# Two distances between the chunks of a matmul operand in SBUF: 2048 and 2080 bytes

## The reference

```python
def ada_in(h, g, m, j):
    xn = rms_norm(h, g)
    return xn * (1.0 + m[:, j, 1][:, None]) + m[:, j, 0][:, None]

def swiglu(x, w_in, w_out):
    a, b = jnp.split(x @ w_in, 2, axis=-1)
    return (jax.nn.silu(a) * b) @ w_out

# second_block, for each of its 2 layers (kind = retention, then neighbourhood attention)
h  = gated_residual(h,  ml, 0, swiglu(ada_in(h,  norm_g[i, 0], ml, 0), ffn_w_in[i, 0], ffn_w_out[i, 0]), 0.5)
hc = gated_residual(hc, mc, 0, swiglu(ada_in(hc, norm_g[i, 0], mc, 0), ffn_w_in[i, 0], ffn_w_out[i, 0]), 0.5)
xl, xc = ada_in(h, norm_g[i, 1], ml, 1), ada_in(hc, norm_g[i, 1], mc, 1)
yl, yc = mixer(xl, xc, ...)          # its input projections are x @ w_in or x @ w_qkv
h  = gated_residual(h, ml, 1, yl, 1.0)
# hc likewise, and a second swiglu, in the last layer for h alone
```

## The kernel before, in words

| | before | remainder by 256 | after | remainder by 256 |
|---|---|---|---|---|
| `xhi`, chunk 0 | 32896 | 128 | 32896 | 128 |
| `xlo`, chunk 0 | 49280 | 128 | 49536 | 128 |
| `raw` and `wlo` | 65664 | 128 | 66176 | 128 |
| `whi` | 82048 | 128 | 82560 | 128 |
| `arena0` (`ghi`, `fhi`, ...) | 129152 | 128 | 130944 | 128 |
| chunk k of `xhi` in block 2 | 32896 + 2048 k | 128 for all k | 32896 + 2080 k | 128 + 32 k, less 256 from k = 4 on |
| chunk k of `xhi` in block 1 | 32896 + 1088 k | 128, 192, 0, 64, 128, ... | same | same |

## Time and profile before

### The profile page before, as it was taken

The page is one execution under the profiler, slowest core; times in us unless marked ns, Lnnn a source line. Parts: engine busy times, 40 slices in busy tenths (PEclk is TensorE's granted clock), DMA queues, the critical chain, the costliest instruction groups (busy, mean ns, idle before and its releaser), DMA issues.

```text
span 3107.7 us, 48774 instructions
## 1 busy us (share of the span) xinstructions
PE 3051.3 (98%) x17714; PEld 2594.2 (83%) x17714; DVE 1880.8 (61%) x3622; ACT 1272.3 (41%) x2142; POOL 204.7 (7%) x350
## 2 busy tenths in 40 slices
PE   9999999999999999999999999999999999999999
PEld 7677899975779998888888888888888888786999
DVE  5555656654567576555676556755557555656554
ACT  4546565343665643222332452322223222336443
POOL 0000000000000010000010000011110111023000
PEclk9999999999999999999999999999999999999999
DMA  5222356622225573444453114445554555462454
GB/s 181 83 76 81 124 174 196 215 95 75 82 89 173 185 238 129 145 148 143 136 190 109 55 62 138 130 150 151 155 161 135 155 158 156 152 178 62 150 182 156
DMA packets 122711, 431.18 MB, mean 139 GB/s; under 512 B 16176, under 2 KB 19504, under 8 KB 122048
## 3 DMA queue, kind: packets, MB, share of 16 engines
q1 hardware_dynamic: 93776, 336.28, 33.0%
q0 software_dynamic: 26880, 86.47, 10.1%
q10 hardware_dynamic: 1904, 6.36, 0.5%
HBM read 427.99 MB, written 8.85 MB: 141 GB/s over the span
## 4 chain that ended last, share of the span: by engine, by line
PE 66%; DVE 1%; ACT 1%; DMA 1%; issue 0%; DVEq 0%; SPq 0%; ACTq 0%
PE ps L429 18%; PE ps L430 18%; PE ps L431 18%; PE ps L510 1%; PE ps L512 1%; PE ps L511 1%; PE ps L922 1%; PE ps L460 1%; PE ps L465 1%; PE ps L461 1%; PE ps L898 1%; PE ps L525 1%; DMA raw<-in_panels 1%; PE ps L981 0%; PE ps L924 0%; PE ps L960 0%
## 5 line engine op out<-in xcount | busy, mean ns | idle before, releaser
L1005 ACT ACTIVATE whi<-raw 128x1024 fp32r<-128x1024 f32 x632 | 668.5, 1058 | 1367.6 <-PE ps L431 854.0
L1576 DVE TENSOR_TENSOR wlo<-raw,whi 128x1024 fp32r<-128x1024 f32 x632 | 773.2, 1224 | 704.3 <-ACT whi L1005 669.7
L429 PE MATMUL ps<-xhi,whi 128*128 128x512 f32 (+2 forms) x2792 | 942.8, 338 | 7.4 <-DVE wlo L1576 7.0
L431 PE MATMUL ps<-xhi,wlo 128*128 128x512 f32 (+2 forms) x2792 | 930.8, 333 | 0.0
L430 PE MATMUL ps<-xlo,whi 128*128 128x512 f32 (+2 forms) x2792 | 930.0, 333 | 0.0
L429 PEld LDWEIGHTS ps<-xhi,whi 128*128 128x128 f32 x2792 | 527.8, 189 | 75.5 <-issue 17.6
L430 PEld LDWEIGHTS ps<-xlo,whi 128*128 128x128 f32 x2792 | 527.8, 189 | 51.2 <-issue 1.0
L431 PEld LDWEIGHTS ps<-xhi,wlo 128*128 128x128 f32 x2792 | 527.9, 189 | 49.6
L387 POOL DMA_DIRECT2D modraw<-in_mod x288 | 155.0, 538 | 2598.1 <-DVE modsum L1683 2414.8
L429 PE MATMUL ps<-ghi,whi 128*128 128x512 f32 (+1 forms) x704 | 255.2, 362 | 0.0
L430 PE MATMUL ps<-glo,whi 128*128 128x512 f32 (+1 forms) x704 | 255.2, 362 | 0.0
(11 more groups left out here) (361 smaller groups left out, 4307.7 us busy)
## 6 DMA issues: line engine op xcount, KB each, us to landing
raw<-in_panels SPq DMA_DIRECT2D x632, 512.0 KB, 3.4
modraw<-in_mod POOLq DMA_DIRECT2D x288, 256.0 KB, 3.0
bias_by_column<-in_rpb POOLq DMA_DIRECT2D x16, 476.2 KB, 8.8
bia<-bias_by_column POOLq DMA_DIRECT2D x32, 96.0 KB, 2.7
rtab<-in_rtab ACTq DMA_DIRECT2D x2, 1312.0 KB, 6.9
wuq<-in_wuq ACTq DMA_DIRECT2D x2, 768.0 KB, 6.5
con<-in_con SPq DMA_DIRECT2D x1, 1345.5 KB, 11.6
h<-in_x SPq DMA_DIRECT2D x1, 1088.0 KB, 6.5
```

The lines of the kernel that those rows point to most:

```text
L429: pe.matmul(out, w_hi, x_hi, start=start, stop=False)
L431: return pe.matmul(out, w_lo, x_hi, start=False, stop=stop)
L1005: act.activation(whi[:, s * PW:(s + 1) * PW], raw[:, s * PW:(s + 1) * PW], ACT.Copy).then_inc(hi_split, 1)
L1576: dve.tensor_tensor(wlo[:, s * PW:(s + 1) * PW], raw[:, s * PW:(s + 1) * PW], whi[:, s * PW:(s + 1) * PW].bitcast(F32), ALU.subtract).then ...
```

## The change: what it does

`X2 = T2 + 8` is the chunk distance of `xhi` and `xlo` in block 2, in floats: 520 floats are 2080 bytes. Both tensors grow by 256 bytes. All that reads or writes them in block 2 uses X2: the norms (which write them), the tiles, the token quarters and the gate panels. Block 1 keeps 1088 bytes. `G2` is T2, so that the chunks of `ghi` and `glo` stay 2048 bytes apart. `steady`, `gsc` and `small` now lie ahead of the area of the stages, `eps` is column 46 of `small`, and everything behind `xlo` has moved up as the table shows. No instruction is added, removed or put elsewhere on any engine.

```diff
+X2, G2 = T2 + 8, T2
...
-        xhi, xlo = sb("xhi", NC * T2, F32R), sb("xlo", NC * T2, F32R)
+        xhi, xlo = sb("xhi", NC * X2, F32R), sb("xlo", NC * X2, F32R)
...
-        modsum, eps = sb("modsum", 8), sb("eps", 1)
-        arena0 = place[0]
-        assert arena0 % 2048 == xhi_at % 2048, (arena0, xhi_at)
-        place[0] += 4 * AW
+        modsum = sb("modsum", 8)
         steady = sb("steady", P)
         gsc = sb("gsc", DEPTH * 3 * NC * 2)
         sm = sb("small", DK + 40)
+        eps = sm[:, 46:47]
+        arena0 = place[0]
+        assert arena0 % 256 == xhi_at % 256, (arena0, xhi_at)
+        place[0] += 4 * AW
...
-        ghi, glo = ar("ghi", 0, FF2 * T2, F32R), ar("glo", FF2 * T2, FF2 * T2, F32R)
+        ghi, glo = ar("ghi", 0, FF2 * G2, F32R), ar("glo", FF2 * G2, FF2 * G2, F32R)
...
             def swiglu_pe(T):
-                tiles(2 * FF2, xhi, xlo, T, T2, first=FIRST)
-                residual_tiles(FF2, ghi, glo, T, T2, ready=part_lo)
+                tiles(2 * FF2, xhi, xlo, T, X2, first=FIRST)
+                residual_tiles(FF2, ghi, glo, T, G2, ready=part_lo)
...
-                tiles(16, xhi, xlo, T2, T2, first=FIRST)
+                tiles(16, xhi, xlo, T2, X2, first=FIRST)
                 tok = [(i * P, P) for i in range(4)]
-                token_tiles(1, tok, T2)
+                token_tiles(1, tok, X2)
...
-                        last = three(bank(b), wh(k), wl(k), xhi[:, k * T2:(k + 1) * T2], xlo[:, k * T2:(k + 1) * T2], k == 0, k == NC - 1)
+                        last = three(bank(b), wh(k), wl(k), xhi[:, k * X2:k * X2 + T2], xlo[:, k * X2:k * X2 + T2], k == 0, k == NC - 1)
...
-                tiles(8, xhi, xlo, NX, T2, first=FIRST)
-                tiles(8, xhi, xlo, T2, T2)
+                tiles(8, xhi, xlo, NX, X2, first=FIRST)
+                tiles(8, xhi, xlo, T2, X2)
...
-                w = T1 if shifts is None else T2
+                w = T1 if shifts is None else X2
...
-                norm(T, gains2(layer, j, T), T2, shifts(layer, j, T))
+                norm(T, gains2(layer, j, T), X2, shifts(layer, j, T))
```

More of the change, by code:

```diff
@@ L224, in build_program @@
         sm = sb("small", DK + 40)
+        eps = sm[:, 46:47]
+        place[0] += 0
+        arena0 = place[0]
+        assert arena0 % 256 == xhi_at % 256, (arena0, xhi_at)
+        place[0] += 4 * AW
+        print("END", place[0], [hex(x) for x in (xhi_at, raw_at, arena0)])
         assert place[0] <= 229368, place[0] - 229368
@@ L254, in build_program @@
         gates_h = nc.alloc_sbuf_tensor_at("gates_h", [P, 7 * T1], F32, offset=xhi_at + 4 * NC * T1)
-        gates_l = nc.alloc_sbuf_tensor_at("gates_l", [P, T1], F32, offset=xhi_at + 4 * (NC * T2 + NC * T1))
+        gates_l = nc.alloc_sbuf_tensor_at("gates_l", [P, T1], F32, offset=xhi_at + 4 * (NC * X2 + NC * T1))
         mrg = ar("mrg", 20 * T1, 4 * T1)
@@ L879, in swiglu_pe @@
             def swiglu_pe(T):
-                tiles(2 * FF2, xhi, xlo, T, T2, first=FIRST)
-                residual_tiles(FF2, ghi, glo, T, T2, ready=part_lo)
+                tiles(2 * FF2, xhi, xlo, T, X2, first=FIRST)
+                residual_tiles(FF2, ghi, glo, T, G2, ready=part_lo)
             def block2():
                 swiglu_pe(T2)
-                tiles(16, xhi, xlo, T2, T2, first=FIRST)
+                tiles(16, xhi, xlo, T2, X2, first=FIRST)
                 tok = [(i * P, P) for i in range(4)]
-                token_tiles(1, tok, T2)
+                token_tiles(1, tok, X2)
                 for q in range(4):
-                    token_quarter((4, 5, 6, 7), q, tok, T2)
-                token_tiles(1, tok, T2)
+                    token_quarter((4, 5, 6, 7), q, tok, X2)
+                token_tiles(1, tok, X2)
                 def ret_scores(r):
@@ L964, in block2 @@
                 for q in range(4):
-                    token_quarter(banks, q, tok, T2)
+                    token_quarter(banks, q, tok, X2)
                     if q == 0:
@@ L1401, in pair @@
                     lane.tile.add()
-                    act.activation(col(ghi, i, T2, T), sq[:, (b // 2) * T2:(b // 2) * T2 + T], ACT.Copy).then_inc(part_hi, 1)
+                    act.activation(col(ghi, i, G2, T), sq[:, (b // 2) * T2:(b // 2) * T2 + T], ACT.Copy).then_inc(part_hi, 1)
                 with lane.loop(2 * FF2 // 4, [(lane.panel, 4), (lane.split, 4), (lane.tile, 4)]) as i:
@@ L2137, in pair @@
                     lane.take(part_hi)
-                    dve.tensor_tensor(col(glo, i, T2, T), w_, col(ghi, i, T2, T).bitcast(F32), ALU.subtract).then_inc(part_lo, 1)
+                    dve.tensor_tensor(col(glo, i, G2, T), w_, col(ghi, i, G2, T).bitcast(F32), ALU.subtract).then_inc(part_lo, 1)
                     lane.count(part_lo).add()
@@ L2164, in block2 @@
                 modulations(0, 1)
-                norm(T2, gains2(0, 1, T2), T2, shifts(0, 1, T2))
+                norm(T2, gains2(0, 1, T2), X2, shifts(0, 1, T2))
                 for i in range(16):
@@ L2304, in block2 @@
                 modulations(1, 1)
-                norm(T2, gains2(1, 1, T2), T2, shifts(1, 1, T2))
+                norm(T2, gains2(1, 1, T2), X2, shifts(1, 1, T2))
                 for i in range(16):
```

## The result

The changed kernel takes 3136.3 us in the median (3135.1 to 3140.6 in four runs) against 3113.6 us for the kernel before (four runs, 3112.0 to 3118.4) on the same chip. The ratio is 1.0075, 95% interval 1.0063 to 1.0087: slower by 22.7 us. The forecast was 3132 us, with a range of 3108 to 3144.

The account below looks back on a forecast made before the run. TensorE, busy for 98% of the span, was taken to bound the kernel. Terms of 15.7 + 2.7 - 1.2 = +17.2 us on 3107.7 gave 3124.9, with 6.8 around the span 3131.7; forecast 3132 us, range 3108 to 3144.

Parts of the forecast that it names:

- the step that read 512-column matmuls by themselves: 512-column rates in the earlier trace: 226.7 ns is the lowest; out of step a matmul starts 3 to 5 ns later.
- Term 1: 512-column matmuls on `xhi`/`xlo` by `three` and `first_tiles`: 4128 x 3.8 ns = +15.7 us, ends 9.1 and 18.2 us.
- the one that explained the cost as settling: 512-column matmuls on `xhi`/`xlo` settle anew at each chunk: 2.2 ns each if short, 4.4 ns if they never settle.
- never settle: Dearer end for 512-column matmuls on `xhi`/`xlo`: they stay out of step, 231.1 - 226.7 = 4.4 ns each.
- Term 2: Token quarters of block 2, 576 matmuls: 4.7 ns dearer each, +2.7 us.
- Term 3: 256-column matmuls on `xhi`/`xlo` in the last stages, 1248: -1.0 ns each, -1.2 us, ends -1.9 and 0.
- Terms 4 and 5: Matmuls on `ghi`, `rhi`, `nhi` and all of block 1; writes at other addresses and moved tensors: 0 us each.
- A (faster): Moving remainders break up a collision of read streams at 512 columns: 3105.5 to 3109.8 us, say 3108; chance 0.18.
- B (nothing): The 512-column rate stays as it is: 3114 us, or 3112 with the 256 columns; chance 0.14.
- its second form: Role, not position, makes block 1's token quarters slow, so no change: 3114 or 3112 us; within the chance of 0.14.
- C: Odd multiples of 32 bytes cost an own fetch in half the chunks: 5952 matmuls, +40 us, 3154; chance 0.05.

Follow-up runs that it names:

- Experiment 2: The kernel before with the weights (raw, wlo, whi) 64 bytes further on, all chunk distances as before: 3147.1 us, ratio 1.0114.
- experiment 1: The changed kernel with X2 = T2, so chunks are 2048 bytes apart again and only the moved tensors differ from the kernel before: 3113.5 us, ratio 0.9996.
- experiments 2 to 4: The kernel before with, in turn, weights 64 bytes further on (3147.1 us), weights 128 bytes further on (3152.3 us), every tensor 64 bytes further on (3116.1 us).

## Why the prediction was right, point by point

**Direction and place** came from the step that read 512-column matmuls by themselves. Had I carried over the 256-column rows, which get faster with moving remainders, I would have forecast a gain. With this change the sign goes with the width, and the profile after has both signs in one kernel: +5.8 ns at 512 columns, -1.6 ns at 256.

**Term 1, `three` and `first_tiles`** was mis-sized. I took 3.8 ns for 4128 matmuls, 15.7 us; 232.5 - 226.7 = 5.8 ns make 23.9 us, above the end of 18.2 that I had given it (the stretch has 862 matmuls, not some 869). The step that failed is the one that explained the cost as settling, with "never settle", 4.4 ns, as its dearest case. Experiment 2 has no step between chunks to settle from and costs 6.5 ns for as long as the stage lasts. The rate while a run settles was a hint on the sign only, and "3 to 5 ns later" does not bound what an offset costs: at rest the seven others cost 2.2 to 7.6 ns. The nearer row was the chunk off by 64 bytes in the earlier trace rows, 233.3 ns, which experiment 2 repeats as a constant rate of 233.2.

**Term 2, token quarters**, was right: 4.7 ns forecast, 232.2 - 226.7 = 5.5 by the stretch, 3.2 us instead of 2.7.

**Term 3, 256 columns**: -1.0 ns forecast, -1.6 ns measured, -2.0 us instead of -1.2.

**Terms 4 and 5, at nothing**, held: `ghi` and block 1 keep their rates, and experiment 1 gives 0.9996 for the moved tensors. It has the area 1280 bytes further on, a change in every remainder by a power of two above 256, and no effect shows; other such shifts were not tried.

The measured terms make 23.9 + 3.2 - 2.0 = +25.1 us, and block 2 grew by 22.6. From start to next start over all matmuls of block 2, the trace gives +23.4, +3.0 and -2.0 us for the three terms. The plain fp32 matmuls, with the pauses behind them, went from 156.4 to 153.8 us, 2.6 less, more than half of it in three pauses after L950 of the kernel before; those on `nhi` took 0.6 us more. Whether the 2.6 us belong to the change or to the one execution is open. So the terms of the prediction were too low by 7 to 8 us. The time was low by only 4.3, and that is luck: 2.6 us went elsewhere, and the three runs that I started from had a median 0.8 us above that of the four.

**The rivals.** A (faster) is true of the 256-column part alone. B (nothing) is refuted by the result, and its second form, that the role and not the position makes the slow matmuls of the earlier trace rows, by experiments 2 to 4: two offsets with the same instructions and the same roles differ by 6.5 ns per matmul. The Trainium skill, "TensorE: Matmul & The Clock Gate", "Step-by-step: what each phase is for", says that loading the next weights takes no SBUF read bandwidth from the running matmul. No run here measures that bandwidth, but the conclusion that I drew from the rule, that addresses could not matter, is wrong: 226.7 against 233.2 ns. Why the relation of the two starts matters is not shown, nor whether it is the load before a matmul or the one beside it that counts. C spoke of odd multiples of 32 bytes as dearer, and that is partly so: 233.2 to 234.3 ns for all four of them, while the even ones have 226.7, 233.2, 232.4 and 228.9. By their means a step of 64 bytes would probably have cost a little less than one of 32; that wasn't tried.

## What to carry to other kernels

In this TensorE-bound kernel of fp32r matmuls, each with a weight load of its own, the start of the stationary operand against the start of the moving one, by remainder by 256 bytes, was worth up to 3.4% of a 512-column matmul (226.7 to 234.3 ns) and 5.7% of one of 256 columns (113.4 to 119.9 ns), without an instruction changed. Measure the distance of starts for each width at rest before choosing a chunk distance, and then keep the relation constant: here 0 for 512 columns, and 64 bytes for 256 in two stages, which gave 0.9944. A rate seen at another width does not even tell the sign.

## What the runs showed of the hardware that I had not expected

- A 512-column fp32r matmul starts 13.4 ns later than its columns take at 2.4 GHz (226.7 against 213.3) at the best offset found and 21.0 ns later at the worst (234.3). At 256 columns it is 6.7 ns (113.4 against 106.7) to 13.2 (119.9).
- The relation is that of stationary minus moving, and is the same when activations and weights change roles (seven pairs, within 1.1 ns by the stretches and 0.1 ns by the means over all starts).
- There can be more than one steady rate for one and the same offset and width: 113.4 and 117.8 ns at 256 columns and 64 bytes.
- A third width goes yet another way. In block 1, with 272 columns and chunks 1088 bytes apart, 412 to 492 us hold 641 or 642 matmuls when the weights lie an odd multiple of 32 bytes further on, against 637 or 638 at the other multiples.
- A mean over the offsets gives the mean of a pattern that goes round them to 0.6 ns (eight offsets) and 1.1 ns (four), but not the single chunk: there it is up to 4.8 ns off.
